# First FFN: eight modulation chunks multiplied and summed on VectorE instead of TensorE, GpSimd's adds one step earlier

## The chip, the cores and the metric

The kernel runs on one core of a Trainium2 chip. The metric is the device time of one execution in microseconds (us), lower is better.

## The reference

Two transformer blocks of two layers each run one after the other in fp32 on 256 tokens of width 1024 (D_FF 2816). The first block carries 256 context tokens beside the 256 latent ones. What matters here is its modulation. For each layer six vectors of width 1024 are made from a condition vector by one large matrix; the latent tokens use the condition `c`, the context tokens `c_ctx`:

```python
m_lat = [m[:, None, :] for m in jnp.split(jax.nn.silu(c) @ ada_w[l] + ada_b[l], 6, axis=-1)]
m_ctx = jnp.split(jax.nn.silu(c_ctx) @ ada_w[l] + ada_b[l], 6, axis=-1)
h_lat = modulate(x_lat, m_lat[0], m_lat[1])
h_ctx = modulate(x_ctx, m_ctx[0], m_ctx[1])
...
f_lat = conv_ffn(modulate(x_lat, m_lat[3], m_lat[4]), ffn_w_up[l], ffn_conv_w[l], ffn_conv_b[l], ffn_w_down[l])
```

Layer 1 needs no context output, so for it the context condition enters only the first two vectors (shift and scale before attention), the latent condition all six. `conv_ffn` multiplies by `w_up`, convolves over three neighbouring tokens, gates and multiplies by `w_down`.

## The kernel before

**Engines and order.** Each engine runs an instruction list written out by hand, with semaphores between them (`Signal`, `Waits`). Weights come in chunks of 128 partitions x 2048 fp32 (1 MB) in one fixed order (`chunk_order`, L108). SP issues their transfers in this order into a ring of four places (`raw`, NRAW = 4, L2953 on): chunk j is issued when chunk j - 4 is no longer needed, and what is behind it in the list waits with it. Chunks of kind "split" are weights of the matrix products: ScalarE rounds them to a high part (`wh`, L1427) and VectorE subtracts it for a low part (`wl`, L1910), in a ring of two places (NSPL = 2), and TensorE multiplies three times, high x high, high x low, low x high (`mm3`, L504 to L506).

**The first FFN** (`up0`) has NT = 22 steps of 128 hidden columns of each half. In step f TensorE makes 48 products of 512 tokens: 24 for part 0 of chunk f, then 24 for part 1 (`hidden`, L739; `ffn`, L777). Three pairs of PSUM banks are used in turn, so step f + 3 waits for the convolution of step f. Beside it, for the same f,

- ScalarE casts the chunk of step f + 2 as soon as TensorE has read chunk f, writes the middle tap of the convolution from PSUM to SBUF (L1624), does the silu of step f - 1 (L1601), and multiplies one modulation chunk by the latent condition, eight products of 128x256 (`ada_products`, L1574, record at L1580), for f < 16.
- VectorE subtracts for the chunk of step f + 2 (L1910), adds the two other taps for both parts (four scalar_tensor_tensor from PSUM, L2275), and in steps 2 to 9 does one pass of the layer norm's affine part on 128x1024 (`affines`, called `spare` here, L2144 and L2147; both operands are in SBUF).
- GpSimd first runs `beside(f)`, then multiplies the two halves of the gate (L2823). `beside` adds the eight products of a modulation chunk to one 128x256 tile in three instructions (`ada_sum`, L2803; L2809 twice, L2812): in step f it takes the chunk that ScalarE multiplied in step f - 1.

**Layer 1's modulation** has 24 chunks of 256 columns. Chunks 8 to 23, which only the latent condition needs, are multiplied on ScalarE and added on GpSimd as above ("sum" chunks, NSUM = 16). What is left to do is to add over the partitions: in the middle of steps 6, 10, 14 and 18 (`SUM_AT`), before part 1, `ada_sums` (L526) does four matrix products with a vector of ones (`onep`) into bank 7; `sum_rows` (L1939), `sums_finish` (L539) and `sum_mods` (L1943) copy, transpose and add the bias around step 19. Chunks 0 to 7, needed for both conditions, are group 6 of `GROUPS`: in the middle of steps 17, 18 and 19 (`ADA_AT`) TensorE multiplies them whole with the two conditions as weights padded to 32 columns (`ada`, L508, record at L520), eight products a chunk, in bank 6; `ada_finish(6)` behind step 20 turns the result with two small products (L553) and `ada_mods` adds the bias. A "raw" chunk frees its place when TensorE has multiplied it.

Of the kernel before, what the change touches and what calls it, by code (L numbers as in the profile page):

```python
# [10 lines left out]
ALU = mybir.AluOpType  # L11
# [49 lines left out]
class Silent:  # L61
# [7 lines left out]
GROUPS = [[(0, c), (0, c + 4)] for c in range(4)] + [[(0, 8 + c) for c in range(8)], [(0, 16 + c) for c in range(8)]]  # L69
GROUPS += [[(1, c) for c in range(8)]]  # L70

ADA_AT = {17: [(6, 0), (6, 1)], 18: [(6, 2), (6, 3), (6, 4)], 19: [(6, 5), (6, 6), (6, 7)]}
FINISH_AT = {20: 6}

# [9 lines left out]
    "hi", "ea", "xh", "exp", "act",  # L84
    "lo", "ev", "xl", "vec", "mods", "conv",
    "lop", "gps", "prod", "affine",
# [3 lines left out]
class Signals:  # L90
    def __init__(self, nc, ctx):
        (self.c, self.cs, self.sel, self.pv, self.bias, self.par, self.x, self.xt0, self.xt1, self.xt2, self.xt3, self.rows, self.rel, self.out, self.raw0, self.raw1, self.raw2,
         self.raw3, self.bt0, self.bt1, self.bt2, self.bt3,
         self.ada, self.adat, self.tr, self.proj, self.score, self.pt, self.val, self.gate, self.gaterow,
         self.hi, self.ea, self.xh, self.exp, self.act,
         self.lo, self.ev, self.xl, self.vec, self.mods, self.conv,
         self.lop, self.gps, self.prod, self.affine) = self.all = [
            Signal(ctx.enter_context(nc.semaphore(f"s_{n}"))) for n in SIGNALS]
        self.raw = [self.raw0, self.raw1, self.raw2, self.raw3]
        self.bt = [self.bt0, self.bt1, self.bt2, self.bt3]  # L100
        self.xt = [self.xt0, self.xt1, self.xt2, self.xt3]
# [6 lines left out]
def chunk_order():  # L108
# [14 lines left out]
    for f in range(NT):  # L123
        o.append(("up0", f, CH, "split"))
        if 0 <= f - 2 < NSUM:
            o.append(("ada1", 8 + f - 2, CH, "sum"))
        o += ada(1, *[i for g, i in ADA_AT.get(f - 1, ())])
    o += [("down0", c, CH, "split") for c in range(NT // 2)]
# [21 lines left out]
def _build(nc, T, ctx):  # L150
# [325 lines left out]
    def tensor_program(e, q):  # L476
# [49 lines left out]
        def ada_sums(j):  # L526

            q.wait_ge(*S.gps.at("onep"))
            if j == 0:
                wait_bank(7)  # L530
            for g in range(4):
                q.wait_ge(*S.gps.at(("adasum", 4 * j + g)))
                m = e.matmul(ps[7][32 * g:32 * g + 32, 0:256], onep[:, 3 - j:35 - j], ADA_SUM[:, j % 2, g, :],
                             start=j == 0, stop=j == 3)
            m.then_inc(*S.ada.up(("sums", j)))
            if j == 3:
                free[7] = [(S.vec, "sumrows")]

        def sums_finish():  # L539

            q.wait_ge(*S.vec.at("sumrows"))
            for f in range(2):
                m = e.transpose(ps[7][:, 128 * f:128 * f + 128], adat[:, 1, 128 * f:128 * f + 128], ident)
            m.then_inc(*S.adat.up("sums"))
            free[7] = [(S.mods, "sums")]

# [230 lines left out]
        def ffn(up, down, first, ngrp, ada_every=False):  # L777
            for f in range(first, NT):
# [12 lines left out]
                for part in range(2) if ngrp == 1 or f < NT - 1 else ():  # L791
                    if part and ada_every:
                        for n_, i in ADA_AT.get(f, ()):
                            ada(n_, i)
                        if f in SUM_AT:
                            ada_sums(SUM_AT[f])
# [3 lines left out]
                hidden_free(up, f)  # L800
                if ada_every and f in FINISH_AT:
                    ada_finish(FINISH_AT[f])
                if ada_every and f == SUM_FINISH:
# [1086 lines left out]
    def vector_program(e, q):  # L1890
# [48 lines left out]
        def sum_rows():  # L1939
            q.wait_ge(*S.ada.at(("sums", 3)))  # L1940
            e.tensor_copy(adat[:, 1, :], ps[7][:, 0:256]).then_inc(*S.vec.up("sumrows"))

        def sum_mods():  # L1943
# [4 lines left out]
            for f in range(2):  # L1948
                e.tensor_tensor(dst[:, f, :, :], src[:, f, :, :], b[:, f, :, :], ALU.add).then_inc(*S.mods.up("sums"))

        def low(key, k):
# [292 lines left out]
        def ffn(up, down, ngrp, conv, others, ada_every=False, spare=None):  # L2244
# [7 lines left out]
            for f in range(NT):  # L2252
                if ada_every and f - 1 in FINISH_AT:
                    ada_mods(FINISH_AT[f - 1])
                if ada_every and f - 1 == SUM_FINISH:
# [23 lines left out]
                if f >= 2 and spare:  # L2279
                    next(spare, None)  # L2280
                if ada_every and f + 1 in FINISH_AT:
                    ada_rows(FINISH_AT[f + 1])
                if ada_every and f + 1 == SUM_FINISH:
# [468 lines left out]
    def gpsimd_program(e, q):  # L2752
# [93 lines left out]
        def block1_ffn(l, ngrp):  # L2846
            def beside(f):
                if f == 12:
                    load_rows(l, 1, [(S.affine, (l, 0, t)) for t in range(2 * ngrp)])
                if l == 0 and 1 <= f <= NSUM:  # L2850
                    ada_sum(f - 1)

# [80 lines left out]
    def sync_program(e, q):  # L2933
# [19 lines left out]
        for j, (name, i, w, kind) in enumerate(ORDER):  # L2953
            if j >= NRAW:
                before = ORDER[j - NRAW]
                if before[3] == "raw":
                    q.wait_ge(*S.ada.at((int(before[0][3]), before[1])))
                elif before[3] == "sum":
                    q.wait_ge(*S.gps.at(("adasum", before[1] - 8)))
                else:  # L2960
                    q.wait_ge(*S.hi.at((j - NRAW, 1)))
                    q.wait_ge(*low_done(j - NRAW))
# [184 lines left out]
```

## Time and profile before

| | us |
|---|---|
| median of 3 runs | 1595.98 |
| lowest, highest | 1594.99, 1597.16 |
| profiled execution | 1594.27 |
| its span, first to last instruction | 1592.9 |

| engine | busy us | share of the span |
|---|---|---|
| PE (TensorE) | 1550.7 | 97% |
| DVE (VectorE) | 1071.9 | 67% |
| ACT (ScalarE) | 882.0 | 55% |
| POOL (GpSimd) | 335.2 | 21% |

The first FFN's steps 2 to 21 lie between about 297 and 531 us of the span. Times in the rows below are from the start of the span. PEclk is the granted TensorE clock as a share of full speed. A row of a timeline has the start, the time from the start to the end of the last of its instructions (us), the engine, the line, the operation, the tiles it writes and reads, their shape, how many instructions are drawn together, and in brackets the idle time of the engine before it with what ended it. TensorE's durations overlap: the pace is the distance between starts.

### The profile page before, as it was taken

The numbers are of one execution on the slowest core, as the hardware profiler recorded it, in microseconds if no ns is written. First come the engines' busy times: TensorE is split into PE (matmuls) and PEld (weight loads), VectorE is DVE, ScalarE is ACT, GpSimd is POOL, SyncE is SP. The second block draws the span as 40 slices with busy tenths as digits, with TensorE's granted clock in tenths as the row PEclk, the third lists the DMA queues.
The fourth block names the chain that finished last, engine by engine and source line by source line (L and its number), as shares of the span: only waits on it lengthen the run. The fifth ranks groups of instructions, "written<-read, shape, count | busy, mean of one in ns | idle before, by whom it ended". The sixth has DMA issues, their size and how long they took to land.

```text
span 1592.9 us, 25617 instructions
## 1 busy us (share of the span) xinstructions
PE 1550.7 (97%) x9990; PEld 1324.1 (83%) x9990; DVE 1071.9 (67%) x1981; ACT 882.0 (55%) x1734; POOL 335.2 (21%) x335
## 2 busy tenths in 40 slices
PE   6999999999999999999999999999999999999998
PEld 4788778988886888887999988878888898788886
DVE  3743766566534525788787767767887667779874
ACT  2423873666642423577455545655766556567663
POOL 0111420356540000112011102232221013312210
PEclk9999999999999999999999999999999999999999
DMA  9767023254657224011456553424555543345551
GB/s 360 287 241 247 21 81 133 80 211 169 243 211 302 83 102 159 23 65 67 181 186 223 186 201 112 157 80 164 188 191 191 183 162 117 133 149 186 185 200 78
DMA packets 46952, 260.37 MB, mean 163 GB/s; under 512 B 11888, under 2 KB 13168, under 8 KB 18160
## 3 DMA queue, kind: packets, MB, share of 16 engines
q1 hardware_dynamic: 43952, 252.78, 43.6%
q0 software_dynamic: 1296, 4.72, 0.8%
q8 instruction: 80, 1.31, 0.3%
q10 hardware_dynamic: 1584, 1.23, 0.3%
q14 instruction: 40, 0.33, 0.1%
HBM read 257.64 MB, written 1.07 MB: 162 GB/s over the span
## 4 chain that ended last, share of the span: by engine, by line
PE 88%; DVE 5%; ACT 4%; DMA 1%; issue 1%; POOL 1%; ACTq 0%; SPq 0%; DVEq 0%
PE ps L504 21%; PE ps L506 21%; PE ps L505 21%; PE ps L756 8%; PE ps L757 5%; PE ps L659 2%; PE ps L681 2%; PE ps L668 2%; PE ps L520 2%; DMA raw<-in_ada 1%; PE ps L758 1%; PE ps L1156 1%; PE ps L567 1%; ACT wh L1427 1%; DVE wl L1916 1%
## 5 line engine op out<-in xcount | busy, mean ns | idle before, releaser
L1910 DVE TENSOR_TENSOR wl<-raw,wh 128x1024 fp32r<-128x1024 f32 (+2 forms) x308 | 359.1, 1208 | 251.7 <-ACT wh L1427 250.3
L1427 ACT CAST wh<-raw 128x1024 fp32r<-128x1024 f32 (+1 forms) x318 | 313.6, 1036 | 323.2 <-PE ps L506 280.2
L504 PE MATMUL ps<-xx,wh 128*128 128x256 f32 (+1 forms) x1006 | 328.4, 326 | 3.3 <-DVE wl L1916 3.2
L506 PE MATMUL ps<-xx,wl 128*128 128x256 f32 (+1 forms) x1006 | 325.5, 324 | 0.0
L505 PE MATMUL ps<-xx,wh 128*128 128x256 f32 (+1 forms) x1006 | 325.5, 324 | 0.0
L504 PE MATMUL ps<-wh,xx 128*128 128x512 f32 (+2 forms) x780 | 285.7, 366 | 2.2 <-issue 0.8
L506 PE MATMUL ps<-wh,xx 128*128 128x512 f32 (+2 forms) x780 | 281.1, 360 | 0.0
L505 PE MATMUL ps<-wl,xx 128*128 128x512 f32 (+2 forms) x780 | 281.0, 360 | 0.0
L2275 DVE SCALAR_TENSOR_TENSOR arena<-ps,pv,arena 128x254 f32<-128x254 f32 (+2 forms) x352 | 193.1, 548 | 28.7 <-ACT arena L1624 19.3
L504 PEld LDWEIGHTS ps<-xx,wh 128*128 128x128 f32 x1006 | 190.1, 189 | 24.3 <-issue 4.4
L506 PEld LDWEIGHTS ps<-xx,wl 128*128 128x128 f32 x1006 | 190.1, 189 | 15.2
L505 PEld LDWEIGHTS ps<-xx,wh 128*128 128x128 f32 x1006 | 190.1, 189 | 14.6
L2823 POOL TENSOR_TENSOR arena<-arena 128x256 f32<-128x256 f32 (+1 forms) x88 | 97.4, 1107 | 487.6 <-ACT arena L1601 487.6
L756 PE MATMUL ps<-xx,wh 128*128 128x512 f32 x504 | 180.8, 398 | 0.0
L504 PEld LDWEIGHTS ps<-wh,xx 128*128 128x128 f32 x780 | 147.1, 189 | 30.1 <-issue 7.8
L506 PEld LDWEIGHTS ps<-wh,xx 128*128 128x128 f32 x780 | 147.1, 189 | 21.7
L505 PEld LDWEIGHTS ps<-wl,xx 128*128 128x128 f32 x780 | 147.3, 189 | 20.5
L757 PE MATMUL ps<-xx,wl 128*128 128x256 f32 x576 | 149.9, 281 | 0.0
L2769 POOL TENSOR_TENSOR st<-st,cs 128x1 f32<-128x1 f32 (+2 forms) x45 | 39.9, 886 | 475.7 <-DVE st L2086 222.3
L1624 ACT ACTIVATE arena<-ps,pv 128x256 f32<-128x256 f32 (+1 forms) x176 | 98.8, 611 | 47.7 <-DVE ps L2265 42.6
L757 PEld LDWEIGHTS ps<-xx,wl 128*128 128x128 f32 x576 | 108.7, 189 | 6.8
L756 PEld LDWEIGHTS ps<-xx,wh 128*128 128x128 f32 x504 | 94.8, 188 | 19.7
(238 smaller groups left out, 2244.2 us busy)
## 6 DMA issues: line engine op xcount, KB each, us to landing
raw<-in_ada SPq DMA_DIRECT2D x48, 1024.0 KB, 5.1
raw<-in_up SPq DMA_DIRECT2D x44, 1024.0 KB, 5.1
raw<-in_fin SPq DMA_DIRECT2D x44, 1024.0 KB, 4.8
raw<-in_down SPq DMA_DIRECT2D x22, 1024.0 KB, 4.9
raw<-in_fout SPq DMA_DIRECT2D x22, 1024.0 KB, 4.9
raw<-in_win SPq DMA_DIRECT2D x12, 1024.0 KB, 4.9
raw<-in_ev_w_in SPq DMA_DIRECT2D x9, 1024.0 KB, 7.7
raw<-in_wout SPq DMA_DIRECT2D x8, 1024.0 KB, 4.8
```

What stands on the lines that cost most here:

```text
L504: e.matmul(out, A[0], B[0], start=first, stop=False)
L505: e.matmul(out, A[0], B[1], start=False, stop=False)
L506: return e.matmul(out, A[1], B[0], start=False, stop=last)
L520: m = e.matmul(ps[b][32 * g:32 * g + 32, 0:256], silp[:, k, 14 - 2 * i:46 - 2 * i], wv[:, k, :], start=(i == 0 and k < 4), stop=(last and ...
L756: e.matmul(both, hv[:, k, fs], xx[:, :, k, 0:256], start=k == 0, stop=False)
L757: m = e.matmul(both[:, 1, :], lv[:, k, fs], xh[:, k, 0:256], start=False, stop=False)
L1427: e.copy(hi_of(j)[:, a:b], raw_of(j)[:, a:b]).then_inc(*S.hi.up((j, half)))
L1624: e.activation(temp(up, f)[:, part, 0:n], ps[2 * (f % 3) + part][:, 0:n], ACT.Identity, bias=w[3], scale=w[1 if up[0] == "u" else 2]).then ...
L1910: e.tensor_tensor(lo_of(j)[:, a:b], raw_of(j)[:, a:b], hi_of(j)[:, a:b].bitcast(F), ALU.subtract).then_inc(*S.lo.up((j, half)))
L2275: e.scalar_tensor_tensor(acc[:, :, lo:hi], src[:, :, lo + shift:hi + shift], conv(row, f + NT * part), acc[:, :, lo:hi], ALU.mult, ALU.add ...
L2769: e.tensor_tensor(out, in_, minus_half[:, 0:n], ALU.pow).then_inc(*S.gps.up(key))
L2823: e.tensor_tensor((ACTF if ngrp == 2 else ACTF1)[:, f, 0:n], t[:, 1, 0:n], t[:, 0, 0:n], ALU.mult).then_inc(*S.prod.up((up, f)))
```

## The change

- `GROUPS` loses its group 6, and TensorE's `ada` calls of steps 17 to 19, `ada_finish(6)`, and VectorE's `ada_rows` and `ada_mods` for it go.
- Chunks 0 to 7 of layer 1 are now of kind "both". They are taken in steps 2, 4, ..., 16 (`BOTH_AT`), and stand in the chunk order two steps behind the "sum" chunk of the same step. VectorE multiplies each by the two conditions, one 128x256 slice at a time, and adds in the same instruction (`ada_both`): 16 instructions, at the end of VectorE's step. Two chunks fill the four tiles `tmp4`; then TensorE adds them over the partitions with four products into bank 6, right behind `ada_sums` of steps 6, 10, 14, 18, and the next chunk waits for that.
- `sum_rows`, `sums_finish` and `sum_mods` treat bank 6 beside bank 7: one more copy, two more transposes, four more additions.
- GpSimd's `beside(f)` adds the chunk that ScalarE multiplies in step f, not that of step f - 1.
- SP waits for `both` before it issues into the place of such a chunk.

```diff
 
 
 GROUPS = [[(0, c), (0, c + 4)] for c in range(4)] + [[(0, 8 + c) for c in range(8)], [(0, 16 + c) for c in range(8)]]
-GROUPS += [[(1, c) for c in range(8)]]
-
-ADA_AT = {17: [(6, 0), (6, 1)], 18: [(6, 2), (6, 3), (6, 4)], 19: [(6, 5), (6, 6), (6, 7)]}
-FINISH_AT = {20: 6}
+
+BOTH_AT = {2 + 2 * i: i for i in range(8)}
 
 NSUM = 16
...
         o.append(("up0", f, CH, "split"))
         if 0 <= f - 2 < NSUM:
             o.append(("ada1", 8 + f - 2, CH, "sum"))
-        o += ada(1, *[i for g, i in ADA_AT.get(f - 1, ())])
+        if f - 2 in BOTH_AT:
+            o.append(("ada1", BOTH_AT[f - 2], CH, "both"))
     o += [("down0", c, CH, "split") for c in range(NT // 2)]
     o += [("od_w_in", i, CH, "split") for i in (4, 0, 1, 2, 3)]
     o += [("od_w_out", c, CH, "split") for c in range(4)]
...
             q.wait_ge(*S.gps.at("onep"))
             if j == 0:
                 wait_bank(7)
+                wait_bank(6)
             for g in range(4):
                 q.wait_ge(*S.gps.at(("adasum", 4 * j + g)))
                 m = e.matmul(ps[7][32 * g:32 * g + 32, 0:256], onep[:, 3 - j:35 - j], ADA_SUM[:, j % 2, g, :],
                              start=j == 0, stop=j == 3)
             m.then_inc(*S.ada.up(("sums", j)))
+            q.wait_ge(*S.both.at(2 * j + 1))
+            for g in range(4):
+                m = e.matmul(ps[6][32 * g:32 * g + 32, 0:256], onep[:, 3 - j:35 - j], tmp4[:, g, :],
+                             start=j == 0, stop=j == 3)
+            m.then_inc(*S.ada.up(("bothsums", j)))
             if j == 3:
-                free[7] = [(S.vec, "sumrows")]
+                free[6] = free[7] = [(S.vec, "sumrows")]
 
         def sums_finish():
 
             q.wait_ge(*S.vec.at("sumrows"))
-            for f in range(2):
-                m = e.transpose(ps[7][:, 128 * f:128 * f + 128], adat[:, 1, 128 * f:128 * f + 128], ident)
+            for b in range(2):
+                for f in range(2):
+                    m = e.transpose(ps[6 + b][:, 128 * f:128 * f + 128], adat[:, b, 128 * f:128 * f + 128], ident)
             m.then_inc(*S.adat.up("sums"))
-            free[7] = [(S.mods, "sums")]
+            free[6] = free[7] = [(S.mods, "sums")]
 
         def ada_finish(n):
 
...
                             m.then_inc(*S.proj.up(("read", up, k)))
                 for part in range(2) if ngrp == 1 or f < NT - 1 else ():
                     if part and ada_every:
-                        for n_, i in ADA_AT.get(f, ()):
-                            ada(n_, i)
                         if f in SUM_AT:
                             ada_sums(SUM_AT[f])
                     wait_bank(2 * (f % 3) + part)
                     m = hidden_beside(up, f, part) if in_halves(up, f) else hidden(up, f, part, 0, 256 * ngrp)
                     m.then_inc(*S.proj.up((up, f, part), ("use", J[up, f])))
                 hidden_free(up, f)
-                if ada_every and f in FINISH_AT:
-                    ada_finish(FINISH_AT[f])
                 if ada_every and f == SUM_FINISH:
                     sums_finish()
 
...
             e.tensor_tensor(dst, src, b.unsqueeze(3).broadcast_to([128, w, 2, 2]), ALU.add).then_inc(*S.mods.up(n))
 
         def sum_rows():
-            q.wait_ge(*S.ada.at(("sums", 3)))
-            e.tensor_copy(adat[:, 1, :], ps[7][:, 0:256]).then_inc(*S.vec.up("sumrows"))
+            q.wait_ge(*S.ada.at(("bothsums", 3)))
+            for b in range(2):
+                e.tensor_copy(adat[:, b, :], ps[6 + b][:, 0:256]).then_inc(*S.vec.up("sumrows"))
 
         def sum_mods():
...
             q.wait_ge(*S.adat.at("sums"))
             for f in range(2):
                 e.tensor_tensor(dst[:, f, :, :], src[:, f, :, :], b[:, f, :, :], ALU.add).then_inc(*S.mods.up("sums"))
+            src = ps[6][:, 0:256].rearrange("p (f n v r) -> p f n v r", f=2, n=2, v=2)[:, :, :, :, 0:4]
+            dst = mods[:, 1, 0:16, :].rearrange("p (j n f) v -> p f n v j", j=4, n=2)
+            b = vec("ada_b", 48, 16).rearrange("p (j n f) -> p f n j", j=4, n=2)
+            for f in range(2):
+                for n in range(2):
+                    e.tensor_tensor(dst[:, f, n, :, :], src[:, f, n, :, :], b[:, f, n, :].unsqueeze(1).broadcast_to([128, 2, 4]),
+                                    ALU.add).then_inc(*S.mods.up("sums"))
+
+        def ada_both(i):
+
+            j, n = J["ada1", i], i % 2
+            wv = raw_of(j).rearrange("p (k n) -> p k n", k=8)
+            q.wait_ge(*S.raw[j % NRAW].at(j))
+            if n == 0 and i:
+                q.wait_ge(*S.ada.at(("bothsums", i // 2 - 1)))
+            for k in range(8):
+                for v in range(2):
+                    acc = tmp4[:, 2 * n + v, :]
+                    if k == 0:
+                        e.tensor_scalar(acc, wv[:, 0, :], sil[:, 0, v:v + 1], None, ALU.mult).then_inc(*S.both.up((i, v, k)))
+                        continue
+                    q.wait_ge(*S.both.at((i, v, k - 1)))
+                    e.scalar_tensor_tensor(acc, wv[:, k, :], sil[:, k, v:v + 1], acc, ALU.mult, ALU.add).then_inc(
+                        *S.both.up((i, v, k), *([i] if (k, v) == (7, 1) else [])))
 
         def low(key, k):
 
...
                                 ALU.subtract).then_inc(*S.xl.up((down, c)))
 
             for f in range(NT):
-                if ada_every and f - 1 in FINISH_AT:
-                    ada_mods(FINISH_AT[f - 1])
                 if ada_every and f - 1 == SUM_FINISH:
                     sum_mods()
                 if ngrp == 1 and f in (6, 10):
...
                         q.wait_ge(*S.conv.last())
                 if f >= 2 and spare:
                     next(spare, None)
-                if ada_every and f + 1 in FINISH_AT:
-                    ada_rows(FINISH_AT[f + 1])
+                if ada_every and f in BOTH_AT:
+                    ada_both(BOTH_AT[f])
                 if ada_every and f + 1 == SUM_FINISH:
                     sum_rows()
             made = [0]
...
             def beside(f):
                 if f == 12:
                     load_rows(l, 1, [(S.affine, (l, 0, t)) for t in range(2 * ngrp)])
-                if l == 0 and 1 <= f <= NSUM:
-                    ada_sum(f - 1)
+                if l == 0 and f < NSUM:
+                    ada_sum(f)
 
             ffn(f"up{l}", ngrp, beside)
             for t in range(2 * ngrp):
...
                 before = ORDER[j - NRAW]
                 if before[3] == "raw":
                     q.wait_ge(*S.ada.at((int(before[0][3]), before[1])))
+                elif before[3] == "both":
+                    q.wait_ge(*S.both.at(before[1]))
                 elif before[3] == "sum":
                     q.wait_ge(*S.gps.at(("adasum", before[1] - 8)))
                 else:

```

## Rows read from the trace of the kernel before

**Rows 1.** The page: shares of the chain of work that ended last.

```profile
PE 88%; DVE 5%; ACT 4%; DMA 1%; issue 1%; POOL 1%; ACTq 0%; SPq 0%; DVEq 0%
```

**Rows 2.** Timeline of ScalarE: step 3's casts, its modulation products, step 4's casts.

```profile
318.86 2.00 ACT L1427 CAST wh<-raw 128x1024 fp32r<-128x1024 f32 x2 [2.48 <-PE ps L506]
...
323.35 3.31 ACT L1580 ACTIVATE raw<-raw,sil 128x256 f32<-128x256 f32 x8 [0.62 <-DMA raw<-in_ada]
329.74 2.00 ACT L1427 CAST wh<-raw 128x1024 fp32r<-128x1024 f32 x2 [3.08 <-PE ps L506]
```

**Rows 3.** Timeline of VectorE: step 3 whole, the splits of steps 5 and 6.

```profile
319.94 2.36 DVE L1910 TENSOR_TENSOR wl<-raw,wh 128x1024 fp32r<-128x1024 f32 x2 [3.28 <-ACT wh L1427]
322.22 3.10 DVE L2275 SCALAR_TENSOR_TENSOR arena<-ps,pv,arena 128x510 f32<-128x510 f32 x4
325.35 2.19 DVE L2147 TENSOR_TENSOR X<-X,arena 128x1024 f32<-128x1024 f32 x1
...
341.70 2.36 DVE L1910 TENSOR_TENSOR wl<-raw,wh 128x1024 fp32r<-128x1024 f32 x2 [3.28 <-ACT wh L1427]
...
353.38 2.36 DVE L1910 TENSOR_TENSOR wl<-raw,wh 128x1024 fp32r<-128x1024 f32 x2 [4.08 <-ACT wh L1427]
```

**Rows 4.** Timeline of GpSimd: step 3, and the adds of step 10.

```profile
322.80 1.30 POOL L2823 TENSOR_TENSOR arena<-arena 128x512 f32<-128x512 f32 x1 [4.17 <-ACT arena L1601]
324.06 4.64 POOL L2809 TENSOR_TENSOR raw<-raw 128x1024 f32<-128x1024 f32 x2
...
401.82 3.76 POOL L2809 TENSOR_TENSOR raw<-raw 128x1024 f32<-128x1024 f32 x2
405.65 0.73 POOL L2812 TENSOR_TENSOR arena<-raw 128x256 f32<-128x256 f32 x1
```

**Rows 5.** Timeline of ScalarE: the casts of steps 16 and 20.

```profile
462.70 2.00 ACT L1427 CAST wh<-raw 128x1024 fp32r<-128x1024 f32 x2 [3.77 <-PE ps L506]
...
519.50 2.00 ACT L1427 CAST wh<-raw 128x1024 fp32r<-128x1024 f32 x2 [7.27 <-PE ps L506]
```

**Rows 6.** Timeline of TensorE: the middle of step 18, first and last rows included.

```profile
480.78 0.39 PE L506 MATMUL ps<-xx,wl 128*128 128x512 f32 x1
481.10 1.07 PE L520 MATMUL ps<-raw,silp 128*32 128x256 f32 x16
...
485.93 1.93 PE L520 MATMUL ps<-raw,silp 128*32 128x256 f32 x16 [2.33 <-DMA raw<-in_ada]
...
488.64 0.54 PE L504 MATMUL ps<-xx,wh 128*128 128x512 f32 x1
```

**Rows 7.** Timeline of TensorE: around the sums of step 6.

```profile
345.58 0.39 PE L506 MATMUL ps<-xx,wl 128*128 128x512 f32 x1
...
346.47 0.50 PE L504 MATMUL ps<-xx,wh 128*128 128x512 f32 x1
```

**Rows 8.** Stretches of 2 us: each engine's busy time, then PEclk, DMA share, GB/s.

```profile
484.00:486.00 2.00, 0.07 (x4) 0.07 (x8) 0.05 (x1) 0.00 (x0) 0.00 (x0) 0.84 0.97 373
486.00:488.00 2.00, 2.00 (x20) 0.91 (x24) 0.00 (x0) 0.00 (x0) 0.00 (x0) 0.50 0.99 410
488.00:490.00 2.00, 2.00 (x14) 1.14 (x7) 0.00 (x0) 0.00 (x0) 0.00 (x0) 0.81 1.05 442
```

**Rows 9.** VectorE, groups by form (count, busy, mean ns), then timeline, second block.

```profile
L2591 DVE SCALAR_TENSOR_TENSOR arena<-arena,st 128x256 f32<-128x256 f32 x12 | 5.7, 477 | 0.0
...
1027.64 0.74 DVE L2591 SCALAR_TENSOR_TENSOR arena<-arena,st 128x128 f32<-128x128 f32 x2
```

**Rows 10.** Timelines of VectorE and GpSimd in two places of later stages.

```profile
963.60 3.12 DVE L2464 SCALAR_TENSOR_TENSOR X<-arena,st 128x512 f32<-128x512 f32 x2
963.53 1.98 POOL L2764 TENSOR_TENSOR wl<-raw,wh 128x832 fp32r<-128x832 f32 x1
...
1039.66 2.31 DVE L2593 TENSOR_SCALAR arena<-arena,st 128x128 f32<-128x128 f32 x2
1036.76 4.72 POOL L2758 TENSOR_TENSOR wl<-raw,wh 128x1024 fp32r<-128x1024 f32 x2
1041.45 0.87 POOL L2906 TENSOR_SCALAR arena<-arena,st 128x128 f32<-128x128 f32 x2
```

More of the change, by code:

```diff
@@ L84 @@
     "hi", "ea", "xh", "exp", "act",
-    "lo", "ev", "xl", "vec", "mods", "conv",
+    "lo", "ev", "xl", "vec", "mods", "conv", "both",
     "lop", "gps", "prod", "affine",
@@ L95, in __init__ @@
          self.hi, self.ea, self.xh, self.exp, self.act,
-         self.lo, self.ev, self.xl, self.vec, self.mods, self.conv,
+         self.lo, self.ev, self.xl, self.vec, self.mods, self.conv, self.both,
          self.lop, self.gps, self.prod, self.affine) = self.all = [
```

## The prediction

> **What bounds the kernel now.** I read the page first: TensorE is busy 97% of the span and holds 88% of the chain that ended last [rows 1]. So only two things move the time: what is taken off or put on TensorE's own stream, and a wait that TensorE gets. The timelines of one step of the first FFN come next. ScalarE's two casts open right behind TensorE's last product of a step, so their starts are TensorE's clock: 318.86 and 329.74, a step of 10.88 us [rows 2]. I call the end of TensorE's step f T(f); step 3 ends at 318.8. In that step VectorE splits the weights of step 5 until T+3.5, convolves until T+6.5, adds one affine row pass, and is idle until the next cast [rows 3]: with 7.7 of 10.88 us used (the affine without its wait, below) it has 3 us to spare in steps 2 to 9, and 5.4 us from step 10, where the affine passes are over. GpSimd multiplies the gate at T+4.0, 1.3 us, and adds the modulation products in three instructions; undisturbed (steps 10 on) these take 2.41 + 1.28, then 0.74 [rows 4]. ScalarE's eight products run until T+7.9, having waited 0.6 for their chunk [rows 2].
>
> **What TensorE loses.** The eight chunks of `ada` in steps 17 to 19 and `ada_finish(6)`. The casts of steps 16 and 20 are 56.80 us apart [rows 5]; four bare steps are 43.52. The batch of sums in step 18 stays: a step with one is 11.68 instead of 10.88, by the starts of the splits 341.70 and 353.38 [rows 3], so 0.80. The transposes of `sums_finish` stay too, about 0.26 (the cast intervals of a plain step and of step 20, 11.14, differ by so much). 56.80 - 43.52 - 0.80 - 0.26 = 12.2. `ada_finish(6)` adds an estimated 0.4, its four records between two weight products in step 21. Together 12.6 us. Not all of this is arithmetic: within step 18 TensorE stands 2.33 us for a chunk, and the products behind it take 1.93 us [rows 6], while the granted clock is 0.84, 0.50, 0.81 in three stretches of 2 us [rows 8]. That is 3.4 us at the lower of the two levels (1.2 instead of 2.4 GHz), 1.7 us of work lost after that one idle stretch. The stand, the chunk traffic and the slow stretch go together.
>
> **What TensorE gains.** 16 products `bothsums`, four behind each batch of sums. The present four cost 0.89 from record to record against 0.23 for two neighbours, so 0.66 [rows 7]; 16 packed ones of `ada` cost about 2.1. The slope gives 0.48 for four more in the same place, 1.9 in all (bound: a batch of its own, 0.8 each, 3.2). Two more transposes 0.15. Without any new wait the balance is -12.6 + 1.9 + 0.15 = -10.5 us.
>
> **What VectorE gains.** `ada_both`: 16 instructions a chunk in even steps 2 to 16, each 128x256, behind the affine pass. The nearest row is a scalar_tensor_tensor with one scalar column and both tensors in SBUF: 0.477 long at 128x256, and a 128x128 and a 128x256 one together take 0.74 [rows 9]. So the next one starts 0.07 before the end: 0.40 each, 0.27 for the two of k = 0 (bound: full length, 0.48). 14 x 0.40 + 2 x 0.27 = 6.2 us a chunk. The waits are on the product before last, done by then: nothing. TensorE wants the result of step 4 in the middle of step 6, behind its four sums, at T(4)+16.8; alone, it would be there at T(4)+13.9. So without GpSimd the whole of VectorE's work is hidden.
>
> **What the two engines do to each other.** This is the term that decides. The affine pass takes 2.19 us [rows 3] where the splits of the same width follow each other at 1.14. It began at 325.35 while GpSimd's add of 324.06 was in flight; that add ended at 326.46, the pass at 327.54, 1.08 later, and GpSimd's second add began then and ended late (two adds 4.64, undisturbed 3.76) [rows 4]. The same in two other places [rows 10]: a scalar_tensor_tensor of X stood through a 1.98 us operation of GpSimd, and at 1039.66 two small operations of VectorE took 2.31: the first until GpSimd's 1036.76 pair was over at 1041.48, the second until the next GpSimd operation was. So one with both operands in SBUF waits for the other engine's whole instruction, and the two take turns, GpSimd getting in between two VectorE instructions. The convolutions, with one operand in PSUM, keep their 3.10 us beside GpSimd and are free of it. All of `ada_both` reads two SBUF operands. The Trainium skill says this too (SBUF — State Buffer, "Who interferes with whom": the shared pair is held for the whole instruction, the other blocks). By that rule, which [rows 3, 4, 10] bear out, the ledger below holds; read instead as a plain slowdown by 1.8 while both work, it would give 8.5 us of waits in place of 24, and 1594.
>
> GpSimd now adds in the products' step, from about T+7.3 (the products no longer wait for their chunk), just as `ada_both` starts. Its three adds hold VectorE up by 2.3 + 1.15 + 0.6 less three gaps of 0.14: 3.6; the gate product, 1.0. The ledger, from T(2): affine done 7.7; `ada_both` own 6.2, adds 3.6, gate product (due at 14.9) 1.0, which makes 18.5; at 18.2 the adds of step 3 begin, the first costs 2.3: done 20.8. Splits of step 3: 2.3, the other two adds 1.6: done 24.7. TensorE's step 5 needs them at T(4) = 21.76: **a wait of 3.0**. Convolution and affine: 29.0 = T(4)+7.3. Step 4: splits and a gate product, 10.6; convolution 13.8; affine 15.3; `ada_both` 6.2, with the last add 0.6, a gate product 1.0 and the adds of step 5, 3.6: done T(4)+26.7. TensorE stands at `bothsums` from T(4) + 3.0 + 10.88 + 5.33 + 0.6 = 19.8: **a wait of 6.9**. In it VectorE catches up, and steps 6 to 9 repeat the pattern: 3.0 and 6.9 again. From step 10 without affine passes `ada_both` ends at T+17.5, then at T+18.7 a pair later; the same ledger leaves 4.3 us over steps 13 to 18. Sum of waits 24.1. The two stands of 6.9 will each bring the lower clock; by the one seen, 1.7 each, 3.4 (bounds 0 and 8, if all five stands do).
>
> The queues that the change touches: SP issues chunks in order, and a `both` chunk frees its place only when VectorE is done, T+21; the `sum` chunk behind it is then there 6 us later (a transfer lands in about 5), T(f+2)+5 at worst, where ScalarE's products want it at T+4: some 1 us of shift, no TensorE time. GpSimd's gate product waits behind the adds, ScalarE's tap of step f+2 for it: done by T+19, wanted at T+22. `sum_rows` and `sum_mods` grow by five small operations on VectorE in steps 18 and 20, where 5 us are free.
>
> **Sum.** -10.5 + 24.1 + 3.4 = +17.0. The profiled execution took 1594.27 (span 1592.9), which gives 1611.3; the median of the runs is 1595.98, 1.7 above it, so **1613.0**.
>
> **The rivals.**
> (1) VectorE keeps the port through its row of products, and GpSimd's adds are what gets later. Then `ada_both` ends at T+13.9, TensorE never waits, and the time is 1595.98 - 10.5 = 1585.5. It decides if GpSimd can't start between two products. For it: instructions of VectorE overlap by 0.07 here. Against: [rows 10]. Chance 0.15.
> (2) The adds slide under the convolutions, which GpSimd doesn't disturb. Of the 12.8 us in the ledger up to step 6, 6.3 can go there at best; the wait in step 6 is then about 1, and the time 1588; with half of it some 4, and 1594. Against: in time, the convolution ends at T+6.5, before the adds. Chance 0.10: 0.03 faster, 0.04 same, 0.03 slower.
> (3) The snowball is larger: products at 0.47 apart (1.1 us more a chunk), so that steps 12 to 18 wait as in 4 to 6, and each stand costs clock: 31 + 6 - 10.5 = +26, 1622. Chance 0.13.
> (4) The forecast, 0.60, its own range 1604 to 1621. The last 0.02: TensorE's part isn't what it says (the chunks' time was load that comes back elsewhere), no change.
> A result within 0.2% of before, about 3 us, is what a measurement of this kernel can't tell from no change. Faster 0.18, same 0.06, slower 0.76. The range: 1592 to 1624, which leaves out (1), 0.15, and some 0.04 above.
>
> **What the new profile would show.** VectorE's 16 products from about T+7.7, some of them 0.5 to 2.5 us long, each with a GpSimd operation under it; `ada_both` some 13 us in steps 2 and 4 instead of 6.2. TensorE idle 7 us before `bothsums` in steps 6 and 10, 3 before steps 5 and 9, and the granted clock at 0.5 behind. No `ada` records in steps 17 to 19, and ScalarE's cast of step 17 with no wait for DMA. I'm wrong if GpSimd's adds are the ones that stretch and VectorE's products stay at 0.40, or if the adds lie under the convolutions.

## The result: 9 us slower, and how the profile after differs

| | before | after |
|---|---|---|
| median of 6 runs each, us | 1596.09 (1594.9 to 1598.1) | 1605.1 (1602.16 to 1608.64) |
| ratio | | 1.0061, 95% interval 1.005 to 1.0072 |
| profiled execution, span, us | 1592.9 | 1600.8 |
| mean granted clock | 0.998 | 0.993 |
| VectorE, GpSimd busy in it, us | 1071.9, 335.2 | 1150.2, 360.8 |

Slower, as forecast, but by 9 us instead of 17. A second series of runs of the changed kernel (below) gave 1.0046 (1.0031 to 1.0061). In what follows, T(f) is the start of ScalarE's first cast behind step f, as in the prediction; a "stand" is a time in which TensorE waits; and `ada_both(f)` is the run of 16 instructions that VectorE does in its step f, whatever the number of the chunk.

The page of after, its chain of work, against [rows 1]:

```profile
PE 84%; DVE 9%; ACT 4%; issue 2%; DMA 1%; POOL 1%; ACTq 0%; DVEq 0%; POOLq 0%; SPq 0%
```

TensorE gave up 4 points of the chain and VectorE took them. The waits of TensorE in the first FFN of after say where (engine, line, what it waited for: us in all, times, longest):

```profile
PE ps L503 <- issue: 7.0, 2, 3.7
PE ps L538 <- DVE tmp L1975: 0.4, 1, 0.4
```

There are two stands of 3.69 and 3.34 us before steps 5 and 9 (put down to "issue" here; TensorE goes on when VectorE's second split of the weights ends), and nothing to speak of at `bothsums` (line 538). The timeline of TensorE at the first of them, then the stretches around both (busy time of PE, PEld, DVE, ACT, POOL, then PEclk, DMA share, GB/s):

```profile
334.08 0.77 PE L503 MATMUL ps<-xx,wh 128*128 128x512 f32 x1 [3.69 <-issue]
```

```profile
327.00:333.00 6.00, 3.39 (x15) 2.46 (x14) 6.00 (x5) 2.52 (x3) 4.27 (x3) 1.00 0.08 11
333.20:340.00 6.80, 5.92 (x14) 4.70 (x15) 6.66 (x7) 3.60 (x9) 1.66 (x1) 0.50 0.99 404
...
384.40:391.20 6.80, 5.95 (x14) 4.73 (x15) 6.66 (x7) 3.95 (x10) 1.66 (x1) 0.50 0.82 325
```

Behind each stand TensorE runs at the lower level, 0.50 of 2.4 GHz, for 6.8 us, of which 5.9 us are after it went on: 3.0 us lost. ScalarE's casts show the same in one number: the step between them takes 17.6 us.

```profile
330.48 1.99 ACT L1429 CAST wh<-raw 128x1024 fp32r<-128x1024 f32 x2 [3.81 <-PE ps L505]
...
348.09 2.00 ACT L1429 CAST wh<-raw 128x1024 fp32r<-128x1024 f32 x2 [7.23 <-PE ps L505]
```

Why VectorE is late there, one timeline each of VectorE and GpSimd shows, behind T(2) = 308.72. The splits at 331.63 are those that step 5 waits for; VectorE's last line is the next chunk, `ada_both(4)`:

```profile
315.97 3.36 DVE L2171 TENSOR_TENSOR X<-arena 128x1024 f32<-128x1024 f32 x1
319.26 2.20 DVE L1972 TENSOR_SCALAR tmp<-raw,sil 128x256 f32<-128x256 f32 x2
321.38 10.33 DVE L1975 SCALAR_TENSOR_TENSOR tmp<-raw,sil,tmp 128x256 f32<-128x256 f32 x14
331.63 2.35 DVE L1912 TENSOR_TENSOR wl<-raw,wh 128x1024 fp32r<-128x1024 f32 x2
...
347.24 5.62 DVE L1975 SCALAR_TENSOR_TENSOR tmp<-raw,sil,tmp 128x256 f32<-128x256 f32 x14
```

```profile
315.86 4.63 POOL L2834 TENSOR_TENSOR raw<-raw 128x1024 f32<-128x1024 f32 x2 [1.78 <-ACT raw L1582]
...
323.55 1.44 POOL L2848 TENSOR_TENSOR arena<-arena 128x512 f32<-128x512 f32 x1 [2.24 <-ACT arena L1603]
326.74 3.82 POOL L2834 TENSOR_TENSOR raw<-raw 128x1024 f32<-128x1024 f32 x2 [1.76 <-ACT raw L1582]
```

`ada_both(2)`'s 14 products take 10.33 us; in the next chunk, with no GpSimd instruction that gets in, the same 14 take 5.62. And the affine pass ahead of it takes 3.36, 1.17 more than in [rows 3]. The two products of k = 0 (line 1972) read only one tensor from SBUF, and they were held as well: 1.38 and 0.90 us here, where undisturbed ones take 0.34.

By ScalarE's casts, step by step against before (in before the cast of step 17 waits for its chunk, so of steps 17 and 18 only the sum counts): step 5 +6.73, step 9 +6.41 (stand and lower clock); steps 6, 10, 18 and 14 +0.47 each for `bothsums`, step 14 another 0.57 for waits; steps 17, 18 and 19 -3.96, -5.30 and -2.96, step 21 -0.49, step 20 +0.23. The sum is +3.1 over the FFN. The span is 7.9 longer: 0.7 more lie before step 2, and 4.1 behind the FFN, of which 3.4 are one stretch of 6.8 us at half clock in the block after it:

```profile
1020.00:1029.40 9.40, 6.81 (x52) 5.93 (x51) 7.52 (x26) 7.83 (x24) 4.59 (x8) 1.00 0.37 119
1029.50:1036.30 6.80, 6.80 (x33) 5.82 (x32) 4.25 (x13) 2.58 (x10) 0.14 (x1) 0.50 0.34 140
```

### The profile page after: what moved, and what is told of

Read it like the earlier page. It is cut to its first block, busy times and chain, and to the rows that moved or that the text cites. A ratio compares the mean times of both kernels' runs of the same rounds, so it can differ in the third digit from the quotient of the medians.

```text
span 1600.8 us, 25553 instructions
## 1 busy us (share of the span) xinstructions
PE 1554.6 (97%) x9892; PEld 1328.3 (83%) x9892; DVE 1150.2 (72%) x2112; ACT 881.5 (55%) x1734; POOL 360.8 (23%) x335
## 3 DMA queue, kind: packets, MB, share of 16 engines
q8 instruction: 79, 1.29, 0.3%
## 4 chain that ended last, share of the span: by engine, by line
PE 84%; DVE 9%; ACT 4%; issue 2%; DMA 1%; POOL 1%; ACTq 0%; DVEq 0%; POOLq 0%; SPq 0%
PE ps L503 20%; PE ps L504 20%; PE ps L505 20%; PE ps L762 8%; PE ps L763 4%; PE ps L665 2%; PE ps L687 2%; PE ps L674 2%; PE ps L519 1%; PE ps L764 1%; DVE tmp L1975 1%; ACT wh L1429 1%; DVE wl L1912 1%; PE ps L1158 1%; ACT arena L1813 1%
## 5 line engine op out<-in xcount | busy, mean ns | idle before, releaser
L1912 DVE TENSOR_TENSOR wl<-raw,wh 128x1024 fp32r<-128x1024 f32 (+2 forms) x308 | 367.5, 1234 | 175.9 <-ACT wh L1429 174.4
L2848 POOL TENSOR_TENSOR arena<-arena 128x256 f32<-128x256 f32 (+1 forms) x88 | 115.3, 1310 | 428.3 <-ACT arena L1603 428.2
```

Source lines behind the costliest of these rows:

```text
L1912: e.tensor_tensor(lo_of(j)[:, a:b], raw_of(j)[:, a:b], hi_of(j)[:, a:b].bitcast(F), ALU.subtract).then_inc(*S.lo.up((j, half)))
L2848: e.tensor_tensor((ACTF if ngrp == 2 else ACTF1)[:, f, 0:n], t[:, 1, 0:n], t[:, 0, 0:n], ALU.mult).then_inc(*S.prod.up((up, f)))
```

## The experiments

My theory after the result: VectorE and GpSimd take turns at SBUF's port, which makes VectorE late; all else follows. Rivals: VectorE's work alone is too much; the step in which GpSimd adds matters by itself; the lower clock is the loss.

**The parts alone.** `shift_only` is the kernel before with this edit alone:

```diff
-                if l == 0 and 1 <= f <= NSUM:
-                    ada_sum(f - 1)
+                if l == 0 and f < NSUM:
+                    ada_sum(f)
```

> The kernel before with one part of the change alone: GpSimd adds the products of step f in step f instead of step f+1. No ada_both, TensorE as before. My theory (VectorE had 3 us a step to spare, and only the affine pass meets the adds): the affine pass is held up by one add, 2.3 us, and ends at T+10, ahead of the next splits; no wait on TensorE, 1596 within 2. Rival (the shift itself makes part of the loss, since splits now meet GpSimd's later adds): 1600 or more, with a wait at TensorE in steps 3 to 9.

Measured: 1592.11 us against 1597.04, ratio 0.9968 (0.9958 to 0.9979), 4.9 us faster; neither theory had that (the first was right that no new wait would come, and 4 us too high). In the trace TensorE has no wait at all in the FFN, where before it had 2.7 us for chunks of `ada`. SyncE's timeline gives the reason (time, duration of issuing, line, transfer, count): the three chunks for step 18 are issued from 468.64 on, 3.6 us behind T(16); in the kernel before from 472.91 on, 10.2 us behind T(16), since GpSimd gives back the buffers of the products a step later there.

```profile
468.64 4.01 SPq L2963 DMA_DIRECT2D raw<-in_ada  x3
```

The products of the three chunks come as one group, with no stand and at full clock, 0.93 us a chunk (for before see [rows 6]):

```profile
483.30 2.80 PE L520 MATMUL ps<-raw,silp 128*32 128x256 f32 x48
```

Steps 17 to 19 take 41.10 us together instead of 45.66: 4.6 of the 12.7 us that the change saves on TensorE can be had by this edit alone.

`adds_late` is the changed kernel with the reverse of that edit.

> The changed kernel with the other part undone: ada_both stays, but GpSimd adds the products of step f-1 in step f, as before. By my ledger (turns at the port) the adds begin at T+5.3 and the gate product stands ahead of or behind them; with VectorE late, adds, gate product and tap wait for one another, and I expect waits in nearly every step: over 1625. Rival (the adds now run under the convolutions, which GpSimd does not disturb): fewer waits, 1588 to 1596. If it comes out near 1605, it does not matter in which step the adds are.

Measured: 1646.78, ratio 1.0316 (1.0293 to 1.0339). The size was right, the reason not: the casts of steps 3 to 16 lie 14.6 to 15.9 us apart, and what waits is ScalarE, for weights. One line of the waits in the FFN of `adds_late`, then one of SyncE's own in `adds_late` and in after:

```profile
ACT wh L1429 <- DMA raw<-in_up: 113.3, 15, 8.8
```

```profile
SPq L2990 <- POOL arena L2837: 208.7, 15, 16.3
```

```profile
SPq L2990 <- POOL arena L2837: 95.8, 14, 10.3
```

SyncE can't issue the next chunk until GpSimd's last add (line 2837) gives a place of the ring back. `psum_late` (below) takes the port out of it.

**Is it GpSimd?** `adds_one`: the changed kernel without two of GpSimd's three adds.

```diff
             q.wait_ge(*S.act.at(("product", 8 + i)))
-            for k in (4, 2):
-                e.tensor_tensor(wv[:, 0:k, :], wv[:, 0:k, :], wv[:, k:2 * k, :], ALU.add).then_inc(*S.gps.up())
-                q.wait_ge(*S.gps.last())
```

> The changed kernel with two of GpSimd's three adds a chunk left out (128x1024 and 128x512; only products 0 and 1 are added, so the modulation of those 16 chunks is incomplete); ada_both and everything on TensorE stay. My theory (the whole loss is what GpSimd's instructions take from VectorE at the port, 3.4 of 4.0 us a chunk, and the clock behind the two stands): no stand before steps 5 and 9, no stretch at half clock there, and TensorE's own balance of -10.6 us remains: 1585.5 within 2. Rival (VectorE's own 6.2 us a chunk are too many): waits stay, 1595 or more.

Measured: 1587.15, ratio 0.9942 (0.9926 to 0.9959). In the FFN TensorE has no wait, its steps are 10.88 and 12.15 us, and there is no stretch at half clock. VectorE's own work is not too much; GpSimd's adds beside it are. (With fewer adds the buffers come back earlier too; `in_psum` keeps all three adds and excludes that as the cause.)

**Is it the port?** `in_psum` moves the running sums out of SBUF; it also puts both kinds of sums over partitions into bank 7 (one copy and two transposes fewer) and waits for `bothsums` only ahead of the last products of a chunk. `in_sbuf` differs from it by one line. Of `in_psum`, against after, the main places:

```diff
-                m = e.matmul(ps[6][32 * g:32 * g + 32, 0:256], onep[:, 3 - j:35 - j], tmp4[:, g, :],
-                             start=j == 0, stop=j == 3)
+                m = e.matmul(ps[7][32 * g:32 * g + 32, 0:256], onep[:, 3 - j:35 - j], tmp4[:, g, :],
+                             start=False, stop=j == 3)
...
-                    acc = tmp4[:, 2 * n + v, :]
+                    acc = ps[6][:, 256 * v:256 * v + 256]
+                    if k == 7 and v == 0 and n == 0 and i:
+                        q.wait_ge(*S.ada.at(("bothsums", i // 2 - 1)))
...
-                    e.scalar_tensor_tensor(acc, wv[:, k, :], sil[:, k, v:v + 1], acc, ALU.mult, ALU.add).then_inc(
+                    e.scalar_tensor_tensor(acc if k < 7 else tmp4[:, 2 * n + v, :], wv[:, k, :], sil[:, k, v:v + 1], acc,
+                                           ALU.mult, ALU.add).then_inc(
```

and `in_sbuf`, against `in_psum`:

```diff
-                    acc = ps[6][:, 256 * v:256 * v + 256]
+                    acc = adat[:, v, :]
```

> The changed kernel with ada_both's two running sums in a PSUM bank instead of SBUF (the last product of each chunk writes to SBUF for TensorE), and both kinds of sums over partitions in one bank, which saves two transposes and a copy. Each of the products then has one operand in SBUF, as the convolutions, which keep their length beside GpSimd. Theory: the products aren't held up by GpSimd any more; only the affine pass and the splits are. What one product costs with PSUM no row shows: at 0.40 apart, as in SBUF, no stands, 1585.5; at 0.48, 1.3 us a chunk more, stands of 2 to 5 us over steps 6 to 10, 1590 to 1595. Rival (it isn't the port of SBUF but GpSimd itself, or VectorE's sheer work, that binds): 1600 or more, and products of 0.5 to 2.6 us with a GpSimd instruction under them.

> The kernel with the running sums in PSUM, with one line changed: the running sums lie in SBUF again (a tile of their own, so that everything else, the merged sums over partitions and the later wait for them too, is as there). If the port of SBUF is the cause, products of 1.4 to 2.6 us come back where a GpSimd instruction is in flight, and the stands before steps 5 and 9 or at bothsums with them: 1600 to 1606. If the gain of 18 us came from the merging of the sums or from the moved wait, this stays below 1590.

Measured: `in_psum` 1586.91 against 1597.01, ratio 0.9941 (0.9924 to 0.9958); `in_sbuf` 1599.21 against 1596.13, 1.0027 (1.0011 to 1.0042). One line makes 12 us, and the FFNs of the two profiles differ by as much. (`in_sbuf` came out 1 us below its forecast and 3.7 below the changed kernel in the same series, `after_again`; its profile lacks the stretch at half clock behind the FFN, which cost 3.4.) VectorE and GpSimd of `in_psum`, the same place as above:

```profile
319.86 0.86 DVE L1969 TENSOR_SCALAR ps<-raw,sil 128x256 f32<-128x256 f32 x2
320.64 4.78 DVE L1972 SCALAR_TENSOR_TENSOR ps<-raw,sil,ps 128x256 f32<-128x256 f32 x12
```

```profile
324.14 1.29 POOL L2846 TENSOR_TENSOR arena<-arena 128x512 f32<-128x512 f32 x1 [2.23 <-ACT arena L1601]
```

12 products take 4.78 us, 0.39 apart, although GpSimd's gate product ran beside them and took its undisturbed 1.29. All 16 products of k = 0 in this trace take 0.47 to 0.49, the two here with GpSimd's adds in flight. And the same place in `in_sbuf`, where the same 12 take 8.04, and the last two 2.37:

```profile
321.59 8.04 DVE L1972 SCALAR_TENSOR_TENSOR adat<-raw,sil,adat 128x256 f32<-128x256 f32 x12
329.55 2.37 DVE L1972 SCALAR_TENSOR_TENSOR tmp<-raw,sil,adat 128x256 f32<-128x256 f32 x2
```

Its stands before steps 5 and 9 are back, 3.69 each. The product in PSUM cost nothing extra, the question that I had left open between 0.40 and 0.48; only the two of k = 0 follow each other at 0.39 instead of 0.26. The Trainium skill has the rule (SBUF — State Buffer, "Who interferes with whom"): an instruction of VectorE with at most one input in SBUF, outside the modes that use both of its ports, does not contend with GpSimd, one with two contends with a GpSimd instruction that reads SBUF. The traces agree for the products of k > 0, 0.39 us apart against up to 2.64 us for one. The products of k = 0 have one input in SBUF and were held all the same where they also wrote to SBUF, up to 2.49 us; undisturbed they take 0.34 there and 0.47 with the result in PSUM, and no run here shows in which mode they ran.

`psum_late` is `in_psum` with GpSimd's adds a step later.

> The kernel with the running sums in PSUM, with GpSimd adding the products of step f-1 in step f, as before the change. In the kernel adds_late (running sums in SBUF) a step took 15.5 us and ScalarE's casts waited for weights, 113 us in all. Theory (the ring of four chunks: a chunk of products that is given back a step later holds its place, and with a chunk for ada_both in every second step the weights come late, whatever the port does): the step of 14 to 15.5 us stays, over 1630. Rival (VectorE's lateness behind the port made the ring late): below 1600.

Measured: 1642.13, ratio 1.0287 (1.0272 to 1.0303): 4.7 us below `adds_late`. The wait for weights is still there, and SyncE waits for GpSimd's last add as in `adds_late` (208.5 us, 15 times), so it is the ring of four chunks, not the port:

```profile
ACT wh L1427 <- DMA raw<-in_up: 112.5, 15, 8.8
```

**Where does the missing stand of 6.9 us come from?** `low_last` lets TensorE do everything in a step that needs no low parts of weights first, and waits for them then:

```diff
...
+                if late:
+                    q.wait_ge(*S.hi.at((J[up, f], 1)))
+                    for part in range(2):
+                        wait_bank(2 * (f % 3) + part)
+                        hidden_high(up, f, part)
+                    q.wait_ge(*low_done(J[up, f]))
...
```

> The changed kernel with TensorE's order inside a step of the first FFN changed: per step first the 32 products that need only the high parts of the weights (both halves), then the wait for the low parts, then the 16 products with them. VectorE, ScalarE and GpSimd as in the changed kernel. The stands before steps 5 and 9 (3.69 and 3.34 us in the trace after) come from the split of the low parts; with 7.1 us of products ahead of that wait they should vanish, and with them the half clock behind them (6.8 us each, 3.4 us lost). What then is left is the wait at bothsums in steps 6 and 10, which the slow clock had covered: ada_both(4) was done at T(4)+22.4, TensorE asks at T(4)+20.4: 2 to 6 us each. So 1596.1 - 10.6 + 4 to 12, 1590 to 1598, more if these stands bring the lower clock too (3.4 each). Rival (the stands only move, the sum is VectorE's overload and stays): 1605.

Measured: 1603.75, ratio 1.005 (1.0031 to 1.0069), what the rival said. The stands before steps 5 and 9 are gone, and two of 6.7 us stand at `bothsums` in steps 6 and 10:

```profile
PE ps L538 <- DVE tmp L2000: 13.4, 2, 6.7
```

That is the 6.9 of the prediction, in a kernel in which T(5) is hardly late (0.75 us): GpSimd's adds of step 5 fall on `ada_both(4)`:

```profile
348.41 9.18 DVE L2000 SCALAR_TENSOR_TENSOR tmp<-raw,sil,tmp 128x256 f32<-128x256 f32 x14
```

`keep_busy` fills the stands of the changed kernel with 14 products each:

```diff
+                if ada_every and f in (5, 9):
+                    q.wait_ge(*S.hi.at((J[up, f], 1)))
+                    wait_bank(2 * (f % 3))
+                    for _ in range(14):
+                        e.matmul(ps[2 * (f % 3)][:, 0:512], hi_of(J[up, f])[:, 0:128], xh[:, 0, 0:512], start=True, stop=True)
```

> The changed kernel, and on TensorE ahead of the wait for the low parts of the weights in steps 5 and 9, 14 products more each (their result is overwritten by the step's own): 14 x 0.227 = 3.2 us of work in the place of the stands of 3.69 and 3.34 us, so that TensorE doesn't stand there and no half clock follows. Theory A (the stretch at half clock costs nothing of its own: VectorE is the bound there, the slow clock delays ScalarE's products and GpSimd's adds of step 5 past ada_both(4), and without it these adds fall on ada_both(4) and TensorE stands at bothsums, as in the kernel with the low parts last, 6.7 us): the half clock behind steps 5 and 9 goes, stands of 4 to 7 us appear at bothsums in steps 6 and 10, the time is 1603 to 1612. Theory B (the half clock is a loss by itself, 3.4 us each): 1596.1 + 9 - 6.8 = 1598.

Measured: 1609.8, ratio 1.0083 (1.0068 to 1.0098). By the time it is theory A: the half clock behind steps 5 and 9 is gone, and the loss isn't (a slow stretch of 6.8 us comes with the stand of step 10 instead). But only one of the two stands at `bothsums` is as large as expected, 6.30 us in step 10; in step 6 it is 1.72. The timelines of GpSimd and VectorE in step 6 and in step 10 show what makes the difference:

```profile
354.71 7.07 POOL L2853 TENSOR_TENSOR arena<-arena 128x512 f32<-128x512 f32 x1 [2.32 <-ACT arena L1608]
361.74 2.40 POOL L2839 TENSOR_TENSOR raw<-raw 128x1024 f32<-128x1024 f32 x1
...
405.37 1.60 POOL L2853 TENSOR_TENSOR arena<-arena 128x512 f32<-128x512 f32 x1 [2.33 <-ACT arena L1608]
408.55 3.89 POOL L2839 TENSOR_TENSOR raw<-raw 128x1024 f32<-128x1024 f32 x2 [1.58 <-ACT raw L1587]
```

```profile
352.73 5.62 DVE L1980 SCALAR_TENSOR_TENSOR tmp<-raw,sil,tmp 128x256 f32<-128x256 f32 x14
...
403.38 10.21 DVE L1980 SCALAR_TENSOR_TENSOR tmp<-raw,sil,tmp 128x256 f32<-128x256 f32 x14
```

At 354.71 GpSimd's gate product did not get the port until VectorE's row of products and the splits behind it were over, 7.07 us for 1.3 of work; the adds queued behind it, and the row ran undisturbed. At 405.37 it got in, and the adds after it too.

**Both remedies.** `in_psum_low` is `in_psum` with the order of `low_last`.

> The kernel with the running sums in PSUM, and on TensorE the low parts of the weights last in each step, as in the kernel low_last. If the running sums in PSUM leave only lateness of the splits, a few us, the 7.1 us of products ahead of the wait for them cover it: no stand at all, TensorE's own balance, 1585 to 1587. If stands at bothsums are left (VectorE late there), 2 to 4 us each, 1589 to 1594.

Measured: 1585.36, ratio 0.993 (0.9915 to 0.9945): the fastest, 11.7 us below the kernel before. `in_psum` had no stand left in the FFN, so the order adds at most little: the intervals overlap, and of the 2.1 us between the two profiled spans some 1.7 are a stretch of 3.4 us at half clock at 959 us, far from the edit, which of the two only `in_psum` has.

**What repeats.** `after_again` is the changed kernel once more.

> The changed kernel once more, for what repeats of its profile. What VectorE sets should repeat: stands of 3.3 to 3.7 us before steps 5 and 9 with 6.8 us at the lower clock behind each, no stand in steps 6 and 10. The stretch at half clock at 1029 us (6.8 us, 3.4 lost) in the block after the FFN: if it is a consequence of the change it repeats; if it is chance it need not, and the time is 3.4 us less without it. 1602 to 1609.

Measured: 1602.9 (1600.65 to 1607.98), ratio 1.0046 (1.0031 to 1.0061). Stands of 3.70 and 3.41 before steps 5 and 9, 6.8 us at half clock behind each, none in steps 6 and 10; and the stretch at half clock came again, from 1028.1 on:

```profile
1028.50:1035.20 6.70, 6.70 (x34) 5.72 (x33) 4.41 (x13) 2.58 (x10) 0.00 (x0) 0.52 0.33 138
```

It follows a stand of TensorE of 1.95 us. `low_last`, `keep_busy`, `adds_one` and `adds_late` have that stand with 1.94, 1.96, 1.94 and 1.94 us and no lower clock behind it, so its length does not decide. Without the change the stand is 1.63 us, in `in_psum` and `in_sbuf` 1.6. That the slow stretch belongs to the change is possible (two traces of two), not shown. Against before, this profile is 3.0 us longer in the FFN and 3.9 behind it, as the first (3.1 and 4.1); ahead of the FFN it is 0.4 shorter, where the first was 0.7 longer.

## Point by point: what held, and the step that failed

- **TensorE's balance, -10.5.** Right: the casts give -12.7 (12.6), +1.9 (1.9) and +0.23 (0.15), -10.6 in all, and `adds_one` shows it by itself, 9.9 us below before. (The 5.4 us that the prediction calls free in a VectorE step from 10 on are 4.4 by the count that gave 3 us for steps 2 to 9; nothing rested on it.) But the prediction took the stand in step 18 and the slow stretch behind it for a property of the chunks on TensorE. `shift_only` shows that 4.6 of it were the adds' place in the order. I had asked what the queue past which they move does to the ring only for the new chunks, not for the old ones, and so counted one gain under the wrong edit.
- **The port.** Right, and the term that decides: instructions with two operands in SBUF wait for GpSimd's whole instruction (a product takes 0.9 to 2.6 us then, instead of 0.48). That all of `ada_both` reads two such operands is wrong for the two products of k = 0, but they were held too. The sum for the end of `ada_both(2)` was T(2)+20.8, measured T(2)+23.0. The adds of step 2, from T(2)+7.1 on, cost 3.8, on the affine pass and the products of k = 0, where the ledger had 3.6. What it lacked is that the last adds of step 1 hold up the splits (0.7), and that all three adds of step 3 fall on `ada_both(2)`, not only the first (1.4, which the ledger had put on the splits behind). At the end of those splits, for which TensorE waits, the difference is only 0.6: T(2)+25.3 for 24.7.
- **The stand before steps 5 and 9.** Forecast were 3.0 us, measured 3.69 and 3.34.
- **The stand of 6.9 at `bothsums`, and the clock.** This is the step that failed. I let the stand of 3.0 cost nothing at the clock, and put 1.7 us behind each of the later stands. (The 1.7 was itself a little too much: of the 3.4 us at half clock in [rows 8], 0.6 lay in the stand, so 1.4 were lost.) In after the stand of 3.7 is followed by 6.8 us at half clock, 3.0 lost, and this makes T(5) 6.7 us late instead of 3.0. ScalarE's products and GpSimd's adds of step 5 come later by as much: the first add starts at 356.26, `ada_both(4)` had ended at 352.87, in time for TensorE. So the slow stretch took the place of the second stand. A group of four steps costs 6.7 and 6.4 us, by my sum 3.0 + 6.9 + 1.7 = 11.6. `low_last`, with no slow stretch before it, shows the 6.9 (6.7 measured) and ends no faster. It isn't the clock alone: in `keep_busy`, where the slow stretch is missing too, the stand came in full only in step 10; in step 6, where GpSimd's gate product was shut out, it was 1.72.
- **GpSimd always gets its turn.** Too simple. In the traces of after, `after_again`, `keep_busy` and `low_last` 28 gate products began while a product of `ada_both` ran; 14 took 1.3 to 1.6 us, and 14 took 4.3 to 7.1: each of these had its last 1.3 us just behind VectorE's row and the two splits that follow, when the convolution, with one operand in PSUM, began. None of the large adds had to wait so. This is the rival (1), true for half of one kind of instruction. What decides it stays open; the time since the start of VectorE's instruction does not (14 to 638 ns in those that got in, 40 to 396 in those that did not).
- **Steps 13 to 18.** Forecast were 4.3 us, measured 0.6. The gate products at 448.0 and 471.6 were shut out, which spares `ada_both` 1.0 each; the rest of the difference I have not accounted for.
- **The sum.** Waits and clock in the FFN 13.7 instead of 27.5; against this, 4.8 us outside it that I had not forecast (0.7 before it, 3.4 of half clock and 0.7 more behind it). -10.6 + 13.7 + 4.8 = +7.9, the difference of the two spans; the 1.1 that the medians differ by beyond it no profile shows (the one after is the fastest of its six executions). So the nearness of 9 to 17 is in part luck: the stage that the forecast is about lost 3.1 us, not 17.0, and more than half of the difference comes from outside it, 0.7 of it not repeated in the second profile and 3.4 not shown to belong to the change.

## What to carry to other kernels

Where VectorE and GpSimd work at the same time, count the operands that each VectorE instruction has in SBUF: moving a running sum to PSUM was worth 12 us here and cost next to nothing, while the work as such fitted in. The count isn't the whole of it, as the products of k = 0 show. A term for the clock is not simply added to a stand: when the late engine is another one, slow products give it time, and one of the two takes the other's place. Ask of every step that moves when it gives its buffer back: the adds' move alone made the kernel before 4.9 us faster, and without it the new chunks starve the weights (50 us above the kernel before).

## What I had not expected of the hardware

- GpSimd's instruction of 1.3 us held off for 7.07 us by a row of 0.48 us instructions and two splits, while in half of the cases it got in at the next boundary. The Trainium skill's section named above says that whoever issues first has the shared pair for the whole instruction. The traces agree for the single instruction (an add of 2.39 us with a product of 2.64 over it); no run here shows what picks the next one.
- The lower clock came in pieces of 3.4 and 6.8 us: 3.4 behind the stand of 2.33 in before [rows 8] and behind those of 3.69 in `in_sbuf`, 6.8 behind those of 3.69 and 3.34 in after. Behind the stands of 6.7 in `low_last` less was lost, 1.6 and 2.4 us, because 3.6 and 2.1 of the slow 6.8 fell into the stand.
- One and the same stand of 2.21 us, late in the program, which all twelve profiles have, was followed by 3.4 us at half clock in five (`shift_only`, `adds_one`, `in_psum`, `keep_busy`, `psum_late`) and by none in seven. A difference of 2 us between two single profiles can be that.
